# Tokens gathered in fp32 for the experts, and a second home for the first pair of up weights

## The reference

```python
logits = (xt @ w_router + b_router).astype(jnp.float32)
top_vals, top_idx = lax.top_k(logits, TOP_K)            # 4 of 32
gates = jax.nn.softmax(top_vals, axis=-1)
...
def expert_block(args):                                 # one block of an expert's tokens
    xb, e = args
    hgu = xb @ w_up_gate[e] + b_up_gate[e]              # 1024 x 2048
    x_glu = jnp.minimum(hgu[:, :D_EXPERT], SWIGLU_LIMIT)
    x_lin = jnp.clip(hgu[:, D_EXPERT:], -SWIGLU_LIMIT, SWIGLU_LIMIT)
    hact = x_glu * jax.nn.sigmoid(SWIGLU_ALPHA * x_glu) * (x_lin + 1.0)
    return hact @ w_down[e] + b_down[e]                 # 1024 x 1024
...
return jnp.zeros((t, d), xt.dtype).at[slot_tok].add(ys * slot_gate[:, None].astype(xt.dtype))
```

## Time and profile before

| | us |
|---|---|
| median of 3 runs | 1586.09 |
| the profiled execution's own time | 1586.05 |
| its span, first to last instruction | 1584.2 |
| TensorE busy | 1457.5 (92%) |
| ScalarE / VectorE / GpSimd busy | 412.2 / 484.5 / 456.7 |
| granted TensorE clock, mean | 0.996 |

### The profile page before, as it was taken

The page is one execution under the profiler, slowest core; times in us unless marked ns, Lnnn a source line. Parts: engine busy times, 40 slices in busy tenths (PEclk is TensorE's granted clock), DMA queues, the critical chain, the costliest instruction groups (busy, mean ns, idle before and its releaser), DMA issues.

```text
span 1584.2 us, 18711 instructions
## 1 busy us (share of the span) xinstructions
PE 1457.5 (92%) x7556; PEld 827.6 (52%) x7557; DVE 484.5 (31%) x848; ACT 412.2 (26%) x521; POOL 456.7 (29%) x353
## 2 busy tenths in 40 slices
PE   8999999988989888989888988889899999999998
PEld 7887433333333333333233333233698776799986
DVE  6536412121121121121121121122567586323211
ACT  6354301011011010010010010011754834453332
POOL 6836000000000000000000000001687754779994
PEclk9999999999999999999999999999999999999999
DMA  9533999999999999999999999999564332545540
GB/s 347 199 116 97 380 428 428 428 427 428 427 428 427 429 427 427 427 428 427 429 427 427 427 427 428 429 427 400 166 213 160 107 106 82 194 150 186 187 160 27
DMA packets 91319, 502.31 MB, mean 317 GB/s; under 512 B 7851, under 2 KB 38179, under 8 KB 66403
## 3 DMA queue, kind: packets, MB, share of 16 engines
q1 hardware_dynamic: 89744, 498.71, 77.9%
q10 hardware_dynamic: 1491, 2.36, 0.5%
HBM read 500.00 MB, written 1.05 MB: 316 GB/s over the span
## 4 chain that ended last, share of the span: by engine, by line
PE 52%; DMA 39%; DVE 3%; ACT 3%; issue 1%; SPq 1%; POOL 1%; DVEq 0%; ACTq 0%
DMA ring<-in_w_up_gate 37%; PE PS L912 13%; PE PS L537 10%; PE PS L539 9%; PE PS L538 9%; PE PS L932 4%; PE PS L939 1%; DMA ring<-in_w_ple_gate 1%; PE PS L879 1%; PE PS L1179 1%; SPq L426 1%; POOL w_low L2362 1%; ACT w_high L1303 1%; DMA ring<-in_w_in 0%; PE PS L921 0%
## 5 line engine op out<-in xcount | busy, mean ns | idle before, releaser
L2362 POOL TENSOR_TENSOR w_low<-ring,w_high 128x512 fp32r<-128x512 f32 x349 | 456.5, 1345 | 1106.3 <-ACT w_high L1303 1105.6
L912 PE MATMUL PS<-ring,arena 128*64 128x512 f32 x2048 | 461.7, 601 | 56.1 <-DMA ring<-in_w_up_gate 56.1
L912 PEld LDWEIGHTS PS<-ring,arena 128*64 128x64 f32 x2048 | 140.9, 137 | 360.6 <-issue 256.9
L932 PE MATMUL PS<-ring,arena 128*64 128x512 f32 x1024 | 227.0, 595 | 28.2 <-ACT arena L1459 28.0
L1450 ACT ACTIVATE arena<-arena 128x512 f32<-128x512 f32 x32 | 20.2, 630 | 756.6 <-DVE arena L1997 756.6
L1303 ACT ACTIVATE w_high<-ring 128x2048 fp32r<-128x2048 f32 (+1 forms) x89 | 166.5, 1881 | 125.8 <-PE PS L539 101.0
L1997 DVE TENSOR_SCALAR arena<-PS 128x512 f32<-128x512 f32 x32 | 22.1, 692 | 466.1 <-PE PS L912 466.1
L932 PEld LDWEIGHTS PS<-ring,arena 128*64 128x64 f32 x1024 | 72.9, 137 | 160.2 <-issue 159.1
L537 PE MATMUL PS<-w_high,XNT_h 128*128 128x512 f32 (+1 forms) x336 | 135.5, 403 | 6.5 <-DVE XNT_l L1710 5.1
L537 PE MATMUL PS<-XNT_h,w_high 128*128 128x256 f32 (+1 forms) x464 | 130.7, 282 | 2.2 <-DVE XNT_l L1693 1.3
L539 PE MATMUL PS<-w_high,XNT_l 128*128 128x512 f32 (+1 forms) x336 | 131.4, 391 | 0.0
(11 more groups left out here) (373 smaller groups left out, 1430.7 us busy)
## 6 DMA issues: line engine op xcount, KB each, us to landing
ring<-in_w_up_gate SPq DMA_DIRECT2D x127, 2048.0 KB, 25.3
ring<-in_w_down SPq DMA_DIRECT2D x64, 2048.0 KB, 23.0
ring<-in_w_in SPq DMA_DIRECT2D x35, 1024.0 KB, 5.4
ring<-in_w_gate_up SPq DMA_DIRECT2D x22, 1024.0 KB, 5.1
ring<-in_w_down SPq DMA_DIRECT2D x11, 1024.0 KB, 4.9
ring<-in_w_out SPq DMA_DIRECT2D x8, 1024.0 KB, 5.0
ring<-in_w_ple_gate SPq DMA_DIRECT2D x4, 1024.0 KB, 22.8
ring<-in_w_ssd_proj SPq DMA_DIRECT2D x4, 1024.0 KB, 5.0
```

Of the source, the lines that this page charges most:

```text
L912: ins = nc.tensor.matmul(PS[64 * (n % 2):64 * (n % 2) + 64, 4 + n // 2, :], x, w[:, n * 512:(n + 1) * 512], start=False, stop=c == KC - 1, ...
L932: ins = nc.tensor.matmul(PS[64 * n:64 * n + 64, 7, :], lhs, w[:, k, n * 512:(n + 1) * 512], start=(j, k) == (0, 0), stop=(j, k) == (1, 3))
L2362: ins = nc.gpsimd.tensor_tensor(LOW[raw_slot(key)][:, at], slot(raw_slot(key))[:, at], HIGH[m % BUF][:, at].bitcast(F32), ALU.subtract)
```

## The change

1. The split copies are gone. ScalarE writes the normed tokens once, in fp32, into `XN`; `token_low` is removed, and with it a later pass of VectorE that wrote the fp32 tokens for the overflow path. `OH4` is fp32.
2. The gather is fp32 and cut by the expert's place in the group. `gather_first` gets the 64 columns of the group's first expert, for all 8 chunks (16 matmuls of 64 columns); `gather_round(q)` gets the other 192 columns for 2 chunks (4 matmuls of 192 columns). Ahead of the loop only `gather_first` is done. A group's rounds now stand inside its own first two experts: rounds 0 and 1 ahead of up chunks 4 and 6 of the first expert, round 2 behind its down products, round 3 ahead of up chunk 2 of the second. The next group's `gather_first` stands ahead of up chunk 2 of the fourth expert.
3. The 16 KB a partition in which the split copies lay are a second home for up pair 0 (`ODD_UP`, semaphore `landed_odd`): odd experts use it, even ones the ring. On SP, up0(1) is issued among the first expert's loads, and up0 of expert e+2 right behind the last load of expert e+1, without waiting for expert e+1.
4. After the experts, the first two `ple_gate` loads wait for expert 30 alone, since expert 31 uses the second home.
5. Semaphores are merged, without effect on the order (`ov_pe`, `ov_act`, `y_mul`, `pos_ps`).

```diff
-        XNH, XNL = pair("XNS", 8192, 10240, 2048)
+        ODD_UP = area(8192, 4096)
...
-            for j in FIRST_EXPERT[2:]:
+            for j in FIRST_EXPERT[2:4]:
                 first_expert(j)
-            with sp.Fori(1, E - 1) as e:
-                expert_loads(e, e)
-            expert_loads(E - 1, E - 1)
+            sp.wait_ge(sem("w_used"), place[("out", 1, 1)] + 1)
+            expert_load(1, 0, odd=True)
+            for j in FIRST_EXPERT[4:]:
+                first_expert(j)
+            with sp.Fori(0, E // 2 - 1) as i:
+                expert_loads(i * 2 + 1, i * 2 + 1, 1)
+                first_up(i * 2 + 2, odd=False)
+                expert_loads(i * 2 + 2, i * 2 + 2, 1)
+                first_up(i * 2 + 3, odd=True)
+            expert_loads(E - 1, E - 1, 1)
...
-            def gather_round(q, bank=6):
+            def gather_first(chunks, bank):
+
+                for c in chunks:
+                    for tb in range(NTB):
+                        ins = nc.tensor.matmul(PS[:, bank, c * CAP:(c + 1) * CAP], XN[:, tb * D + c * P:tb * D + (c + 1) * P],
+                                               OH4[:, tb * 256:tb * 256 + CAP], start=tb == 0, stop=tb == 1)
+                return ins
+
+            def gather_round(q):
 
                 for c in (2 * q, 2 * q + 1):
                     for tb in range(NTB):
-                        for part in (XNH, XNL):
-                            ins = nc.tensor.matmul(PS[:, bank, (c % 2) * 256:(c % 2) * 256 + 256], part[:, tb * D + c * P:tb * D + (c + 1) * P],
-                                                   OH4[:, tb * 256:(tb + 1) * 256],
-                                                   start=(tb, part is XNH) == (0, True), stop=(tb, part is XNL) == (1, True))
+                        ins = nc.tensor.matmul(PS[:, 6, (c % 2) * 256 + CAP:(c % 2 + 1) * 256], XN[:, tb * D + c * P:tb * D + (c + 1) * P],
+                                               OH4[:, tb * 256 + CAP:(tb + 1) * 256], start=tb == 0, stop=tb == 1)
                 ins.then_inc(sem("gathered"), 1)
...
                     for c in range(KC):
-                        if q == 0 and c == 6:
-                            pe.wait_ge(sem("x_slots"), e + 4)
-                        up_chunk(e, c, x[:, c * 256 + q * CAP:c * 256 + (q + 1) * CAP], True)
+                        if q == 0 and c in (0, 4):
+                            pe.wait_ge(sem("x_slots"), rounds + (c // 4 + 1))
+                        if q == 0 and c == 4:
+                            gather_round(0)
+                        elif q == 0 and c == 6:
+                            pe.wait_ge(sem("x_slots"), rounds + 3)
+                            gather_round(1)
+                        elif q == 1 and c == 2:
+                            pe.wait_ge(sem("x_slots"), rounds + 5)
+                            gather_round(3)
...
+                        elif q == 3 and c == 2:
+                            pe.wait_ge(sem("onehot"), i * 2 + (u // GROUP + 2))
+                            gather_first(range(KC), 6).then_inc(sem("gathered"), 2)
...
                     down(e)
                     if q == 0:
-                        pe.wait_ge(sem("onehot"), i * 2 + (u // GROUP + 2))
-                    gather_round(q)
+                        gather_round(2)
```

More of the change, by code:

```diff
@@ L191, in landed_by, with rounds_in @@
         before = sum(1 for k in keys if raw_slot(k) == s and number[k] <= number[key])
-        return 16 * (before + (ROUNDS if number[key] >= late and s in EXPERT_SLOT else 0))
+        return 16 * (before + (rounds_in(s) if number[key] >= late and s in EXPERT_SLOT else 0))
+    def rounds_in(s):
+        return ROUNDS - E // 2 if s == EXPERT_SLOT[0] else ROUNDS
     def slot_fills(s):
@@ L457, in expert_load, with expert_loads, first_up @@
                     src = w_down_e[e, (j - UPS) * 512:(j - UPS + 1) * 512, :].rearrange("(p k) n -> p (k n)", p=P)
-                sp.dma_start(slots2(EXPERT_SLOT[j]), src).then_inc(landed[EXPERT_SLOT[j]], 16)
-            def expert_loads(e, turn):
-                for j in range(PER_EXPERT):
+                if odd and j == 0:
+                    sp.dma_start(ODD_UP, src).then_inc(landed_odd, 16)
+                else:
+                    sp.dma_start(slots2(EXPERT_SLOT[j]), src).then_inc(landed[EXPERT_SLOT[j]], 16)
+            def expert_loads(e, turn, first=0):
+                for j in range(first, PER_EXPERT):
                     sp.wait_ge(sem("w_used"), turn * PER_EXPERT + (before_experts - PER_EXPERT + j + 1))
                     expert_load(e, j)
+            def first_up(e, odd):
+                sp.wait_ge(sem("w_used"), e * PER_EXPERT + (before_experts - 2 * PER_EXPERT + 1))
+                expert_load(e, 0, odd)
             sp.sem_inc(sem("last_half"), 16 * (E - 1))
@@ L941, in scatter @@
                 ins.then_inc(sem(sig), 1)
-            pe.wait_ge(sem("xn_low"), 2)
+            pe.wait_ge(sem("tokens"), 2)
             pe.wait_ge(sem("onehot"), 1)
-            for q in range(4):
-                if q == 3:
-                    pe.wait_ge(sem("gT"), 1)
-                gather_round(q, FIRST_ROUNDS[q])
-                if q == 0:
-                    pe.wait_ge(sem("side_sb"), 3)
-                    for b in range(3):
-                        nc.tensor.matmul(PS[:, b, :], SEL, BUP[:, 0:512], start=True, stop=False, skip_group_check=True)
+            gather_first(range(4), 6).then_inc(sem("gathered"), 1)
+            pe.wait_ge(sem("gT"), 1)
+            gather_first(range(4, KC), 7).then_inc(sem("gathered"), 1)
+            pe.wait_ge(sem("side_sb"), 3)
+            for b in range(3):
+                ins = nc.tensor.matmul(PS[:, b, :], SEL, BUP[:, 0:512], start=True, stop=False, skip_group_check=True)
+            ins.then_inc(sem("sums_biased"), 1)
             pe.wait_ge(sem("late_in"), LATE_IN)
@@ L976, in _ @@
                     pe.wait_ge(sem("h_done"), e + 1)
-                    pe.wait_ge(sem("x_slots"), e + 4)
+                    if q == 0:
+                        pe.wait_ge(sem("x_slots"), rounds + 4)
+                    elif q == 3:
+                        pe.wait_ge(sem("x_slots"), rounds + (ROUNDS_IN + 2))
                     h_transposes("hT_ps")
@@ L1972, in _ @@
             group_one_hots(0)
-            for q in range(4):
-                dve.wait_ge(sem("gathered"), q + 1)
-                group_round_out(XG[0], q, FIRST_ROUNDS[q])
-                if q == 1:
-                    select(0).then_inc(sem("sel"), 1)
+            for half in range(2):
+                dve.wait_ge(sem("gathered"), half + 1)
+                group_first_out(XG[0], half, 6 + half)
+            dve.wait_ge(sem("sums_biased"), 1)
+            select(0).then_inc(sem("sel"), 1)
             for p in range(PASSES - 1):
@@ L1991, in _ @@
                     q, e = u % GROUP, i * (2 * GROUP) + u
-                    if q == 0:
-                        group_one_hots(e + GROUP)
+                    rounds = i * (2 * ROUNDS_IN) + u // GROUP * ROUNDS_IN
                     one_hot_weighted(e, 0, slots0)
                     one_hot_weighted(e, 1, slots0).then_inc(sem("weighted"), 1)
+                    if q == 0:
+                        for r in range(2):
+                            dve.wait_ge(sem("gathered"), rounds + (r + 3))
+                            group_round_out(XG[u // GROUP], r)
+                    elif q == 1:
+                        dve.wait_ge(sem("gathered"), rounds + 6)
+                        group_round_out(XG[u // GROUP], 3)
+                        group_one_hots(e + (GROUP - 1))
+                    elif q == 3:
+                        dve.wait_ge(sem("gathered"), rounds + (ROUNDS_IN + 2))
+                        for half in range(2):
+                            group_first_out(XG[(u // GROUP + 1) % 2], half)
                     dve.wait_ge(sem("up_first"), e + 1)
```

117 lines of the change are left out of this document (61 added, 56 removed).

## The result

The changed kernel takes 1591.36 us (median of 13 runs, 1589.13 to 1598.21); the kernel before took 1587.43 beside it. The ratio is 1.0033, with a 95% interval of 1.0023 to 1.0043: slower by about 5 us by the ratio, by 3.9 between the medians, where 1586.2 was forecast. In a second series it was 1.0049 [1.0032, 1.0066]. Of these 25 runs 11 lie above 1595 and the others between 1588.7 and 1594.1; the upper ones (the kernel before has 2 of 131 there) have a cause of their own, which the fourth group of experiments looks for. The profiled execution is one of the lower kind: 1591.45, a span of 1589.6, 5.4 more than the profiled execution of before.

What follows compares the result with a forecast made beforehand. The prediction took the DMA's stream of 2 MB loads (about 428 GB/s) as the bound, with the end moving with the stream's end. It added 0.15 to 1586.05 for 1586.2 us, range 1583.2 to 1589.2.

Steps and rivals of the forecast that it cites:

- S: Start of the expert loop on TensorE: forecast at 174.1 us, earlier by 0.3 than the 174.44 before.
- the gather (3.75 for 3.5): First gather ahead of the loop: 32 instructions of 64 columns at 0.108 each, forecast 3.5 us.
- the round: A gather step of 4 fp32 matmuls of 192 columns inside the experts: forecast 1.6 us, bounds 0.9 to 2.3.
- the filled spell: First dry spell of the DMA, 165.2 to 168.2, 1.5 us lost before; up0(1), issued earlier, was to fill it.
- the one near 181: Second dry spell of the DMA, before up1(1) is issued at 181.4: forecast to stay; it lost 2.8 us before.
- 0.162: Price in us per instruction of a 192-column matmul, taken half way between 0.108 and 0.216; eight make 1.3 us.
- The gating load: down0(1), expert 1's first down half: forecast issued at 198.95 into an empty queue, landing at 206.65, with down1(1) at 211.55.
- +0.15: Forecast net delay in us of down1(1)'s landing: first dry spell filled, second kept, a third added.
- its 7.7: Time in us from issue to landing for a 2 MB load meeting an empty queue; a queued one adds 4.9.
- The tail: Last expert and after: `gather_first` adds about a microsecond, covered by the DMA wait; the 1.05 us round behind it goes.
- the slow one: Rival: rounds of 2.5 us make expert 0 late, delaying down1(1) by 1.95 and up1(2) by 1.35; 1589.35 us, chance 0.11.
- The fast one: Rival: the loop starts at 170.5, so the queue never runs dry and 4.3 us of spells go; 1581.8 us, chance 0.13.

Runs made afterwards that it cites:

- the fourth group of experiments: Experiments on the runs near 1597: the changed kernel profiled again (1595.34 us), and the changed kernel with the three biases ahead of the first gather (1589.71 us).
- up0_ahead: Changed kernel with the first up pair of the expert after next issued on SP ahead of the next expert's second pair; median 1589.54 us, ratio 1.0010.
- gather_early: Changed kernel with the next group's first gather in a group's third expert instead of the fourth; ratio 1.0038.
- pad_exit: Changed kernel with 120 more semaphore increments at the start of TensorE's program, moving all its code by 120 places; 1603.05 us, ratio 1.0098.
- biases_first: Changed kernel with the three biases of TensorE's sums ahead of the first gather and the first SEL written during it; 1589.71 us, ratio 1.0011.
- all_and_biases: Changed kernel with up0 loads issued ahead, next group's first gather in the third expert, 9 double-width filler matmuls and biases before the first gather; 1586.17 us, ratio 0.9989.
- best: Changed kernel with up0 loads issued ahead, next group's first gather in the third expert, biases before the first gather and 24 start instructions; 1586.79 us, ratio 0.9990.

## Why the prediction was wrong

*The start, right.* S, the gather (3.75 for 3.5), the round, the filled spell, the one near 181 and the issue of `down0(1)` came within 0.3 us. For the round that is in part luck: 0.162 is the price half way between the two rows, at 160 columns, not at 192, and no row shows the 0.3 or 0.15 for a change between half and whole array. The 1.50 measured is 8 x 0.1875, near the 0.18 that a straight line gives at 192 columns, with next to nothing left for two changes. Two slips carry no weight: the fifth slice of the earlier trace rows has 380 GB/s, not 427 to 429, for the dry spells lie in it, and the terms given for expert 1's up products add up to 204.4.

*The gating load, mis-sized.* "up3(1) 9.8 later at 198.9" took the queue at full rate once `up1(1)` was under way; that load itself landed at 189.2, as forecast. The next two loads are issued when the one before still has 2.6 and 4.0 us to go, and follow it by 6.4 and 5.9 instead of 4.9; `up3(1)` lands at 201.4. +0.15 became +1.0; *up0_ahead*, with one more load queued, has 422 and 376 GB/s in the two stretches. Why a load alone in the queue goes slower is not shown. The 2.0 us that the prediction sets beside its 7.7 is, in the Trainium skill (DMA: Bandwidth & Descriptors, Anatomy of one DMA), the fit for DMAs that GpSimd issues; these loads go out on SP's queue. Another 1.2 comes from a gap of 6.4 us between two landings at 232 to 238. The kernel before has four gaps of 5.9 to 6.1 us in the full stream, the changed one five of 6.4 to 6.6, at other places; their cause is open. *gather_early* has the same loads without that gap, and its down products end 1.4 late, so this part of the 2.2 may be chance.

*The tail, the step that failed.* "In the last expert `gather_first` delays TensorE by about a microsecond more, but its last down half waits for the DMA anyway": the microsecond was right (1.1), the cover was not. The row for it has a wait of 0.20, and expert 31's waits add up to 1.34, less than the gather's 3.7. So the end did not move with the stream's end but with TensorE, and *gather_early* shows it: without the gather the wait for the down half is back. The next clause, "the round of 1.05 us behind it is gone", counted as a gain what had lain beside the write of the slots. Nor did I see that the code behind the loop might not be there: the jump of 6.1 us, and *pad_exit* without it, show that this, not the round, makes the 1.97 us.

*Not in the sum at all: the clock.* The stop of 0.77 us ahead of the first gather stood in my account of S as time alone; in the run where the clock falls behind it, expert 0's third pair starts 4.7 us later. In the profiled execution it doesn't fall there, but at the scatter (0.7 us) and at 1146 (1.4).

Of the rivals, the slow one comes near in time (1589.35) by the wrong mechanism: a round is 1.5 us, not 2.5. The fast one's filled spells are nearly what *up0_ahead* does to the stream, which ends 3.3 us before that of the kernel before, with S where it was: it was the order on SP's queue, not S, that decided.

## What to carry to other kernels

Before a cost is called hidden, add up the waits that are to hide it, in the iteration that ends last: 1.34 us of waits cannot hide 3.7. A loop that prepares the next round does so in its last iteration too, for nobody; move such work to an iteration with waits behind it. A second buffer pays by when it is filled: the load whose home is free goes ahead of those that still wait for theirs.

## What was not expected of the hardware

- In the changed kernel and eleven variants the first matmul behind the loop came 2.51 to 2.63 us after a fetch of code, whatever stood before it, and 0.05 to 0.06 after the end of a jump of 3.9 to 6.2 us; 120 instructions more at the other end of the program took the wait away and left a jump of 0.34.
- TensorE's clock fell to half within a gather of 64 columns that followed a stop of 0.76 to 0.77 us, in both profiled runs near 1595, and stayed there for about 10 us; the first profiled execution of the changed kernel has the same stop and gather at full clock. 11 of 25 runs of the changed kernel lie above 1595; of the 33 of *biases_first*, *all_and_biases* and *best* none is above 1591.21 or has a mean clock under 0.993.
- Two 2 MB loads that for a while were alone in the queue took 9.1 and 9.8 us and left the DMA at 369 and 301 GB/s, where the full stream has 428.
- 120 increments of a semaphore hold TensorE from 0.8 to 19.1 us, about 0.15 each.
